# Retrieval stage: one-hot compares issued as scalar-tensor-tensor, and the one-hot sum split into four pairwise additions

## The reference, cut to what matters

```python
v1, i1 = lax.top_k(s1, PEER_TOPK)
v2, i2 = lax.top_k(s2, PEER_TOPK)
cand = (v1[..., :, None] + v2[..., None, :]).reshape(nb, PEER_HEADS, PEER_TOPK * PEER_TOPK)
cidx = (i1[..., :, None] * PEER_N_KEYS + i2[..., None, :]).reshape(...)
sc, sel = lax.top_k(cand, PEER_TOPK)
idx = jnp.take_along_axis(cidx, sel, axis=-1)
g = jax.nn.softmax(sc, axis=-1)
h = jnp.einsum('nd,nhkd->nhk', xb, u[idx])
a = jax.nn.gelu(h) * g
return jnp.einsum('nhk,nhkd->nd', a, v[idx])
```

## Time and profile before

| | before |
|---|---|
| median of 3 runs | 4929.05 us (4917.19 to 4929.27) |
| the profiled execution: time, span of its instructions | 4900.19 us, 4898.4 us |
| TensorE matmul busy | 4146.3 us (85%) |
| VectorE busy | 3165.0 us (65%) |
| ScalarE busy | 1272.6 us (26%) |
| GpSimd busy | 626.6 us (13%) |
| mean granted TensorE clock | 0.887 |

### The profile page before, as it was taken

How to read it: one execution, slowest core, us unless ns; L and a number is a source line. 1 busy time by engine, 2 the same in 40 slices (tenths; PEclk the granted TensorE clock), 3 DMA queues, 4 the chain that set the end, 5 groups by cost and what they waited for, 6 DMA issues and landing times. The chain is left out here.

```text
span 4898.4 us, 61601 instructions
## 1 busy us (share of the span) xinstructions
PE 4146.3 (85%) x20219; PEld 3468.1 (71%) x20219; DVE 3165.0 (65%) x5709; ACT 1272.6 (26%) x2699; POOL 626.6 (13%) x505
## 2 busy tenths in 40 slices
PE   6999798998887875355542899999999999999996
PEld 5788565875444665254442788999999999999995
DVE  4301343111111209999997789999999999999986
ACT  3111232111111211244433222222222222222222
POOL 0000000000000000133333211111111111111110
PEclk9999676556999977688877899999999999999998
DMA  4322321002004010011222777877877778777774
GB/s 137 114 90 79 90 59 39 19 19 89 31 26 155 0 39 5 5 73 73 90 116 94 271 272 269 281 280 271 281 272 272 281 277 280 276 275 286 273 269 168
DMA packets 308268, 770.86 MB, mean 157 GB/s; under 512 B 29121, under 2 KB 170945, under 8 KB 257729
## 3 DMA queue, kind: packets, MB, share of 16 engines
q0 software_dynamic: 55360, 403.60, 22.2%
q1 hardware_dynamic: 233376, 356.77, 21.8%
q10 hardware_dynamic: 19440, 9.44, 0.7%
HBM read 681.01 MB, written 89.78 MB: 157 GB/s over the span
## 5 line engine op out<-in xcount | busy, mean ns | idle before, releaser
L2078 PE MATMUL exp_h<-exp_xh,exp_uh 128*128 128x384 f32 x2048 | 690.5, 337 | 57.5 <-DVE exp_xl L2048 47.5
L2080 PE MATMUL exp_h<-exp_xh,exp_ul 128*128 128x384 f32 x2048 | 688.6, 336 | 0.0
L2079 PE MATMUL exp_h<-exp_xl,exp_uh 128*128 128x384 f32 x2048 | 687.8, 336 | 0.0
L2092 PE MATMUL exp_y<-exp_vh,exp_ah 128*128 128x512 f32 x1536 | 599.2, 390 | 10.5 <-DVE H L1983 10.5
L1900 POOL DMA_INDIRECT exp_uv<-in_peer_uv,gidx x384 | 374.1, 974 | 1795.4 <-DVE H L2010 1757.3
L2094 PE MATMUL exp_y<-exp_vh,exp_al 128*128 128x512 f32 x1536 | 601.6, 392 | 0.0
L2093 PE MATMUL exp_y<-exp_vl,exp_ah 128*128 128x512 f32 x1536 | 601.3, 391 | 0.0
L2004 DVE SCALAR_TENSOR_TENSOR exp_uv<-exp_uv,exp_gx 128x1024 f32<-128x1024 f32 x384 | 469.4, 1223 | 92.6 <-DMA exp_uv<-in_peer_uv,gidx 69.5
L2010 DVE SCALAR_TENSOR_TENSOR H<-exp_uv,exp_coef,H 128x1024 f32<-128x1024 f32 x384 | 491.1, 1279 | 24.0 <-ACT exp_coef L1945 24.0
L1983 DVE TENSOR_TENSOR H<-H,exp_y 128x512 f32<-128x512 f32 x768 | 490.0, 678 | 4.0 <-PE exp_y L2094 3.9
L1936 ACT ACTIVATE exp_ah<-exp_prod 128x384 fp32r<-128x384 f32 x256 | 132.4, 517 | 1353.0 <-DVE exp_prod L1993 1353.0
(11 more groups left out here) (276 smaller groups left out, 6285.5 us busy)
## 6 DMA issues: line engine op xcount, KB each, us to landing
exp_u<-in_peer_u SPq DMA_DIRECT2D x128, 512.0 KB, 4.9
exp_v<-in_peer_v SPq DMA_DIRECT2D x128, 512.0 KB, 4.1
exp_w<-s_w SPq DMA_DIRECT2D x128, 384.0 KB, 3.7
out_z<-proj_zs SPq DMA_DIRECT2D x72, 256.0 KB, 2.0
proj_w<-in_w_in SPq DMA_DIRECT2D x16, 1024.0 KB, 5.5
merge_gates<-out_z SPq DMA_DIRECT2D x9, 1024.0 KB, 5.1
s_zt<-proj_zt ACTq DMA_DIRECT2D x27, 256.0 KB, 2.3
exp_uv<-in_peer_uv,gidx POOLq DMA_INDIRECT x384, 5.7
```

What stands on the lines that cost most here:

```text
L2078: pe.matmul(hp[c][:, 0:TC], uh[s][:, n, :], xh[:, n, at], start=(n == 0), stop=False)
L2079: pe.matmul(hp[c][:, 0:TC], uh[s][:, n, :], xl[:, n, at], start=False, stop=False)
L2080: last = pe.matmul(hp[c][:, 0:TC], ul[s][:, n, :], xh[:, n, at], start=False, stop=(n == KD - 1))
L2092: pe.matmul(yp[x][:, :], ah[a + n][:, rows], vh[half][:, n, :], start=(n == 0), stop=False)
```

## The change

The sum over the 16 rows of `hot` becomes three additions of halves in place (rows 0 to 7 plus rows 8 to 15, then 4 plus 4, 2 plus 2) and a last one into `picked`, with a drain after each of the first three. The two compares of `spread` become scalar-tensor-tensor operations that first multiply in0 by 1.0 and then compare. Operands, types, waits and increments stay; nothing changes its place.

```diff
-                        dve.tensor_reduce(picked[:, a, :], hot[:, :, :].rearrange("p j c -> p c j"), AXX, ALU.add)
+                        for n in (8, 4, 2):
+                            dve.tensor_tensor(hot[:, 0:n, :], hot[:, 0:n, :], hot[:, n:2 * n, :], ALU.add)
+                            dve.drain()
+                        dve.tensor_tensor(picked[:, a, :], hot[:, 0, :], hot[:, 1, :], ALU.add)
...
-                        dve.tensor_tensor(bare[r][:, :, :], key_of[:, :, :], over(key2t[:, bass.ds(b * OH, OH)], NKEY),
-                                          ALU.is_equal).then_inc(bare_ready, 1)
+                        dve.scalar_tensor_tensor(out=bare[r][:, :, :], in0=key_of[:, :, :], scalar=1.0,
+                                                 in1=over(key2t[:, bass.ds(b * OH, OH)], NKEY),
+                                                 op0=ALU.mult, op1=ALU.is_equal).then_inc(bare_ready, 1)
...
-                        dve.tensor_tensor(left[r][:, :, :], over(iota[:, :], OH), along(key1t[:, bass.ds(b * OH, OH)], NKEY),
-                                          ALU.is_equal).then_inc(left_ready, 1)
+                        dve.scalar_tensor_tensor(out=left[r][:, :, :], in0=over(iota[:, :], OH), scalar=1.0,
+                                                 in1=along(key1t[:, bass.ds(b * OH, OH)], NKEY),
+                                                 op0=ALU.mult, op1=ALU.is_equal).then_inc(left_ready, 1)
```

## The result

The changed kernel took 4935.23 us in the median of 20 runs (4907.78 to 4956.02), the kernel before, run beside it, 4920.33 us in 20 (4896.61 to 4935.64). The ratio of the two kernels over all these runs is put at 1.0036, with a 95% interval of 1.0023 to 1.0049: slower by 18 us of 4920, with 11 to 24 as the interval's ends (the two medians are 14.9 us apart). The forecast was plus 17 us and a time of 4946 us, 11 above the measured one. 9 of those 11 us are the base: the 17 was put on 4929, the median of three runs, and 20 runs of the kernel before have their median at 4920.

A forecast was written before the change was run, and what follows sets the result against it. The retrieval phase was taken as a serial chain on VectorE, which takes turns with GpSimd in spread batches. Plus 48.6 for compares minus 31.5 for the sum gave plus 17 on 4929: 4946 us, range 4894 to 4965.

The forecast's parts named there:

- What bounds the stage: Spread batches: VectorE and GpSimd take turns, so scaling 1.69, second keys 0.55 and first keys 1.14 sum to 3.38 us.
- Part 1, the one-hot sum: Strided sum in all nine tiles: additions and drains take 1.86 us, saving 1.75 us 18 times, minus 31.5 us.
- Part 2, second keys: Second-key compare in spread: scalar-tensor-tensor loses the doubled bf16 rate, plus 0.54 us each; batch becomes 3.92 us.
- The argument from the indirect DMA: GpSimd's indirect DMA ends 0.81 us after either VectorE form, so scalar-tensor-tensor with two SBUF operands also holds GpSimd up.
- Part 3, first keys: First-key compare in spread: fp32 before and after, 1.21 us against 1.223, plus 0.01 us each.
- Absorption at the start: First five batches of each spread tile: waiting for TensorE's start absorbs 0.7 of 2.7 us, leaving 8.1 per tile.
- the 8 us that the prediction named as its sign: Each tile's spread should grow by 8 us; a 3.92 us period without that growth would mean mis-sized absorption.
- plus 48.6: Cost of the two changed compares in spread: 8.1 us per tile after absorption, over six tiles.
- 1 (bf16 at the doubled rate): Second-key compare keeps the doubled rate; both compares cost at most 1 us, the sum saving stays: 4899 us; 9%.
- 2 (the new form runs beside GpSimd): Steady batches: new compares neither wait for nor stop scaling, ScalarE's 2.85 us becomes the bound: about 4847 us; 9%.
- 3: One-hot sum: in-place additions do not double their rate, saving only 14 us: 4964 us; 4%.
- 4: First-key compare: two fp32 sources halve its rate, 1.07 us more each, 103 us in all: 5049 us; 2%.

The follow-up runs named there:

- e11_psum_second: e9_first_psum with the second-key compare as scalar-tensor-tensor from SBUF; ratio 0.9930 to the kernel before.
- e1_sums: The kernel before with the four pairwise additions alone, compares unchanged; ratio 0.9935.
- e7_second_act7: The kernel before with 7 of 8 rows scaled on ScalarE instead of 2, and second keys as scalar-tensor-tensor; whole time 5023 us, one execution.
- e2_second: The kernel before with the second-key compare alone as scalar-tensor-tensor; ratio 1.0094.
- e3_first: The kernel before with the first-key compare alone as scalar-tensor-tensor, fp32 in and out; ratio 0.9990.
- e9_first_psum: e1_sums with the first-key compare reading its keys from PSUM, their copy to SBUF dropped; ratio 0.9826 to the kernel before.
- e10_both_psum: e9_first_psum with the second-key compare also reading its keys from PSUM, their copy dropped; ratio 0.9787 to the kernel before.
- e12_psum_act1: e10_both_psum with one row moved from ScalarE back to GpSimd, leaving 1 on ScalarE; ratio 0.9770 to the kernel before.

## Why the prediction was right, by its steps

**What bounds the stage.** Shown. The batch is scaling plus second keys plus first keys: a row less on GpSimd, twice the time of a compare, or an operand moved out of the turn each moved the batch as the sum had it, but for the handover to TensorE in e11_psum_second.

**Part 1, the one-hot sum.** Right in kind, too large in size: 31.5 us forecast, 28.8 in e1_sums. The four additions and three drains were put at 1.86 us and take 1.93 from the first's start to the last's end, against 3.608: 30.3 us over the 18. (The 2.00 of the slot has the drain behind them too, as the 3.65 of the old sum has.) The cause is the 0.68 for 1024 elements, a compare at its shortest; the addition took 0.693. The line through 1.225 and 0.693 gives 0.427 and 0.294 for the next two, and 0.425 and 0.293 were measured, so the doubled rate holds down to 256 elements. The other 1.5 us were not lost in the sums. In e1_sums VectorE's find-index instructions ahead of them, which no edit touched, took 0.16 to 0.37 us more per tile from start to start; why is open.

**Part 2, second keys.** The taken value was 0.54 us, the measured one 0.53: 1210 against 676 ns at the shortest, 1.08 against 0.55 after the scaling, and a batch of 3.90 against the 3.92 forecast. The argument from the indirect DMA, that this form holds GpSimd up like the other, came out, on a narrow base: only 2 of the 384 indirect DMAs start under a scalar-tensor-tensor. **Part 3, first keys.** Forecast plus 0.01 us, measured nothing (1212 against 1211 ns).

**Absorption at the start.** Forecast 0.7 us per tile, and right: in the tile that the prediction follows, the fifth second-key compare ends 13.65 us after the first one's start before and 15.67 in the changed kernel, 2.0 later, as forecast. The change's stretch less that of e1_sums is 834.8 - 788.7 = 46.1 us against 48.6. Of the missing 2.5, about 1.4 is the batch, which grew by 0.53 where 0.55 was forecast, over the 11 batches behind the fifth compare in six tiles. Most of the rest is one of the six tiles of the changed kernel, whose last first-key compare was not held up by a scaling and took 1.2 us instead of the 2.8 of the others. The starts of a tile's first second-key and last first-key compare are 51.8 us apart before and 59.7 after, which is the 8 us that the prediction named as its sign.

So plus 48.6 was 46.1, minus 31.5 was 28.8, and the errors nearly cancelled: 17.1 forecast, 17.3 in the stretch. That it came so close is luck. **The rivals:** 1 (bf16 at the doubled rate) falls by the 1226 ns of e7_second_act7; 2 (the new form runs beside GpSimd) by e2_second and e11_psum_second, though its aim, compares beside the scaling, was reachable by another way; 3 falls by the 693 ns of the first addition, 4 by e3_first. The chance of over 0.3% was given as 0.58, and the measured 0.36% has an interval that reaches down to 0.23%, so this could not have been called more firmly.

## What to carry to other kernels

An instruction's recorded time can be mostly standing: compare its shortest with its median, and see whether its end keeps a fixed distance to the end of an instruction on another engine; where it does, add the two engines' times instead of taking the larger. When two engines take turns at one memory, moving one operand to another memory can be worth more than a faster operation: here the keys in PSUM took 74 us off e1_sums, though the second-key compare then ran at half its rate. And when a change joins two edits and comes out near zero, run each alone: one of them may be worth keeping.

## What the runs showed that I had not expected

The compare costs the same with a broadcast operand in PSUM as in SBUF, 1208 (e9_first_psum) and 1214 ns (e10_both_psum) against 1211 for 1024 fp32 elements. The way out stood in the trace of the kernel before: 122 of the 384 indirect DMAs start under a tensor-tensor with both operands in SBUF (line 2000), take 1.01 us and end 0.81 after it, while 255 start under one with an operand in PSUM (line 1983) and take 0.94, what one takes with nothing running. In e12_psum_act1 some batches still take 2.7 us though no engine's own load asks for more than about 2.3. And the stages that no edit touched vary by up to 28 us ahead of the stretch and 31 behind it from one profile to the next, more than the whole effect that was to be measured.
